# Second gated layer of a two-block transformer kernel on one core: 20 of its 22 feature blocks by seven block products of 256-token halves

## The reference, cut to what matters

```python
def swiglu(h, w1, w3, w2):                     # w1, w3: 1024 x 2816, w2: 2816 x 1024
    return (silu(h @ w1) * (h @ w3)) @ w2
x = x + 0.5 * m_l[2] * swiglu(modulate(rms_norm(x, norm1_w), ...), ffn1_w1, ffn1_w3, ffn1_w2)   # first gated layer
...                                            # token mixing
x = x + 0.5 * m_l[8] * swiglu(modulate(rms_norm(x, norm3_w), ...), ffn2_w1, ffn2_w3, ffn2_w2)   # second gated layer
...                                            # a second block follows
```

## Time and profile before

| | |
|---|---|
| median of 3 runs | 2056.03 us (2053.0 to 2056.21) |
| the profiled execution | 2053.71 us, its span 2051.9 us (1.8 us lie around it) |
| TensorE busy | 95% of the span |
| VectorE, ScalarE, GpSimd busy | 51%, 41%, 41% |
| first gated layer's pairs | about 155 to 550 us |
| norm ahead of the second gated layer | about 969 to 982 us |
| second gated layer | 972.4 to about 1350 us; its last group's down phase ends it |

### The profile page before, as it was taken

The page is one execution under the profiler, slowest core; times in us unless marked ns, Lnnn a source line. Parts: engine busy times, 40 slices in busy tenths (PEclk is TensorE's granted clock), DMA queues, the critical chain, the costliest instruction groups (busy, mean ns, idle before and its releaser), DMA issues.

```text
span 2051.9 us, 25703 instructions
## 1 busy us (share of the span) xinstructions
PE 1945.4 (95%) x9378; PEld 1628.4 (79%) x9378; DVE 1039.4 (51%) x1563; ACT 834.2 (41%) x1276; POOL 836.5 (41%) x414
## 2 busy tenths in 40 slices
PE   4999999999989999889999999999979989999998
PEld 2999999999978875557888888877745767888886
DVE  3879877557457215965213112578985362121124
ACT  4524242434354235552532333446655454232231
POOL 1337574556424321442443443533612324443432
PEclk8999999999999999889999999999989999999999
DMA  8134343433212120002232232322311212232321
GB/s 350 52 134 139 130 163 110 158 143 115 103 62 83 62 71 31 11 21 88 82 112 92 92 108 87 107 98 83 121 44 42 82 51 83 92 113 82 112 82 62
DMA packets 53487, 197.67 MB, mean 96 GB/s; under 512 B 6320, under 2 KB 7056, under 8 KB 51600
## 3 DMA queue, kind: packets, MB, share of 16 engines
q1 hardware_dynamic: 52240, 191.47, 26.6%
q10 hardware_dynamic: 1152, 4.92, 0.7%
HBM read 194.27 MB, written 2.10 MB: 96 GB/s over the span
## 4 chain that ended last, share of the span: by engine, by line
PE 60%; issue 18%; DVE 10%; POOL 7%; ACT 4%; DMA 1%; SPq 0%; POOLq 0%; DVEq 0%; ACTq 0%
PE ps L2276 26%; PE ps L2405 13%; PE ps L2442 8%; POOL wlo L649 6%; PE ps L2290 2%; PE ps L2631 1%; PE ps L2265 1%; PE ps L2264 1%; PE ps L2263 1%; PE ps L2622 1%; PE ps L2789 1%; PE ps L2805 1%; PE ps L2779 1%; DVE ada_prod L1412 1%; DVE rg_h L2178 1%
## 5 line engine op out<-in xcount | busy, mean ns | idle before, releaser
L649 POOL TENSOR_TENSOR wlo<-raw,whi 128x1024 fp32r<-128x1024 f32 x244 | 602.7, 2481 | 991.9 <-ACT whi L702 968.1
L2276 PE MATMUL ps<-h_hi,whi 128*128 128x512 f32 (+2 forms) x992 | 362.3, 380 | 4.5 <-POOL wlo L649 1.8
L702 ACT ACTIVATE whi<-raw 128x1024 fp32r<-128x1024 f32 x244 | 253.1, 1053 | 272.9 <-PE ps L2276 188.3
L2276 PE MATMUL ps<-h_hi,wlo 128*128 128x512 f32 (+2 forms) x992 | 359.7, 377 | 0.0
L2276 PE MATMUL ps<-h_lo,whi 128*128 128x512 f32 (+2 forms) x992 | 359.1, 376 | 0.0
L2276 PEld LDWEIGHTS ps<-h_hi,whi 128*128 128x128 f32 x992 | 182.8, 188 | 43.1 <-issue 8.3
L656 POOL TENSOR_TENSOR wlo<-raw,whi 128x512 fp32r<-128x512 f32 x108 | 160.6, 1501 | 133.2 <-ACT whi L870 132.8
L2276 PEld LDWEIGHTS ps<-h_lo,whi 128*128 128x128 f32 x992 | 182.3, 188 | 33.5 <-issue 1.0
L2276 PEld LDWEIGHTS ps<-h_hi,wlo 128*128 128x128 f32 x992 | 182.4, 188 | 32.7
L2276 PE MATMUL ps<-g_hi,whi 128*128 128x512 f32 x432 | 168.1, 389 | 0.0
L2276 PE MATMUL ps<-g_lo,whi 128*128 128x512 f32 x432 | 168.1, 389 | 0.0
(11 more groups left out here) (476 smaller groups left out, 3690.7 us busy)
## 6 DMA issues: line engine op xcount, KB each, us to landing
raw<-panels SPq DMA_DIRECT2D x280, 512.0 KB, 3.7
ada_w<-ada_t SPq DMA_DIRECT2D x56, 512.0 KB, 3.9
ada_f<-ada_p SPq DMA_DIRECT2D x8, 1024.0 KB, 17.4
x_lat<-x_t SPq DMA_DIRECT2D x1, 2048.0 KB, 7.9
out<-x_lat SPq DMA_DIRECT2D x8, 256.0 KB, 2.2
x_ctx<-ctx_t SPq DMA_DIRECT2D x1, 1024.0 KB, 10.0
cond_b<-cond SPq DMA_DIRECT2D x1, 1024.0 KB, 21.9
x_ctx<-mem_t ACTq DMA_DIRECT2D x1, 1024.0 KB, 4.8
```

The lines of the kernel that those rows point to most:

```text
L649: pool.tensor_tensor(wlo[:, sl], raw[:, sl], whi[:, sl].bitcast(f32), ALU.subtract).then_inc(lo_done, 1)
L702: act.activation(whi[:, sl], raw[:, sl], ACT.Copy).then_inc(hi_done, 1)
L2276: ins = pe.matmul(bank(banks + b, n), wt[:, w], a[:, at_(kc, c0):at_(kc, c0) + n], start=kc == 0 and j == 0, stop=kc == n_k - 1 and j == 2)
```

## The change

Blocks 2 to 21 of the second gated layer go by seven block products of 256-token halves; blocks 0 and 1 (`plain`) stay as they were. What is new beside the reuse of the first layer's functions:

- the norm ahead of the layer also writes the input unrounded, `h32_2` (ScalarE, 8 more instructions), and rounds two panels in its midst;
- VectorE forms differences of token halves from it (16 instructions of 256 columns), ScalarE rounds them (4 of 768), VectorE makes their low parts (4 of 768); another set, `t4_2`, takes the place of the late token halves in `h_hi` and `h_lo` once the plain blocks are done;
- of a block's seven low parts VectorE makes two, 3 and 5 (`vector_low`), and GpSimd five;
- VectorE's additions in the down phases and its work for the later stages are interleaved with weight sums of the next group's first block; the loops are written out.

In the diff `act` is ScalarE, `dve` VectorE, `pool` GpSimd, `pe` TensorE.

```diff
+HALF2 = LAT // 2
+PLAIN2 = 2
+L2_PAIRS = (FF_GROUPS[0] - PLAIN2,) + FF_GROUPS[1:]
+VECTOR_LOW = (3, 5)
...
             def low_operand(m, j):
+                if m >= PAIRS and j in VECTOR_LOW:
+                    pool.wait_ge(s_lo, 6 * m + j)
+                    pool.sem_inc(s_lo, 1)
+                    return
...
-            low_part(2, P_WOUT + 2)
-            low_part(3, P_WOUT + 3)
-            with pool.Fori(P_WOUT // RING + 1, N_PANELS // RING) as i:
+            for p in range(P_WOUT + 2, P_FFN2 + 2 * PLAIN2):
+                low_part(p % RING, p)
+            for n in range(len(L2_PAIRS)):
+                for m in range(PAIR2[n], PAIR2[n] + L2_PAIRS[n]):
+                    for j in range(7):
+                        low_operand(m, j)
+                for d in range(KC):
+                    low_part(d % RING, P_FFN2 + L2_UP[n] + 2 * FF_GROUPS[n] + d)
...
+                    elif m.n == 2 and kc in (3, 4):
+                        q = P_FFN2 + kc - 1
+                        round_panel(q % RING, q // RING + 1, q - RING)
...
+            def second_layer():
...
+                token_sums(0)
+                token_sums(1)
+                plain(0)
+                token_sums(2)
+                token_sums(3)
+                for j in range(3):
+                    round_operand(PAIRS, j)
+                plain(1)
+                act.wait_ge(panel_done, done(P_FFN2 + 2 * PLAIN2 - 1))
+                for e in range(2):
+                    act.activation(late_halves2(h_hi, e), ...).then_inc(t4_rounded, 1)
+                for j in range(3, 7):
+                    round_operand(PAIRS, j)
+                for n in range(len(L2_PAIRS)):
+                    for m in range(PAIR2[n], PAIR2[n] + L2_PAIRS[n]):
+                        pair_products(m)
...
+                    for q in range(down + RING, down + KC):
+                        round_panel(q % RING, q // RING + 1, q - RING)
+                        if q == down + RING:
+                            memory_squares() if n == 0 else memory_hi()
+                    for j in range(7):
+                        round_operand(PAIR2[n + 1], j)
...
+            def vector_low(m, e):
+                j = VECTOR_LOW[e]
+                dve.wait_ge(s_hi, 6 * m + j + 1)
+                dve.tensor_tensor(half_slot(wlo, j), operand(m, j), half_slot(whi, j).bitcast(f32), ALU.subtract).then_inc(v_lo, 1)
...
+            def second_layer():
...
+                differences(0, 2)
+                plain(0)
+                differences(2, 4)
+                weight_sums(PAIRS, 0)
+                sums_low(0)
+                sums_low(1)
+                weight_sums(PAIRS, 1)
+                sums_low(2)
+                sums_low(3)
+                plain(1)
...
+                weight_sums(PAIRS, 2)
+                vector_low(PAIRS, 1)
+                for n in range(len(L2_PAIRS)):
+                    for m in range(PAIR2[n], PAIR2[n] + L2_PAIRS[n]):
+                        if pair_unit(m):
+                            pair_tail(m - 1)
+                        if not last_pair(m):
+                            weight_sums(m + 1, 0)
+                            weight_sums(m + 1, 1)
+                        pair_sums_of(m)
+                        if not last_pair(m):
+                            vector_low(m + 1, 1)
...
             def first_products(m):
...
                 if m == 0:
                     pe.wait_ge(t_ready, 4)
+                elif m == PAIRS:
+                    pe.wait_ge(t_ready, 8)
...
+            def second_layer():
+                cols = token_cols(LAT)
+                first_pair(P_FFN2, (0, 2), H_BEFORE[2], cols)
...
+                for n, g in enumerate(FF_GROUPS):
+                    for m in range(PAIR2[n], PAIR2[n] + L2_PAIRS[n]):
+                        first_products(m)
```

More of the change, by code:

```diff
@@ L50 @@
 PAIRS = FF - L1_SIZES[0]
+HALF2 = LAT // 2
+PLAIN2 = 2
+L2_PAIRS = (FF_GROUPS[0] - PLAIN2,) + FF_GROUPS[1:]
+VECTOR_LOW = (3, 5)
+PAIR2 = [PAIRS + sum(L2_PAIRS[:n]) for n in range(len(L2_PAIRS))]
+PAIRS2 = PAIRS + sum(L2_PAIRS)
+L2_UP = [sum(2 * g + KC for g in FF_GROUPS[:n]) for n in range(len(FF_GROUPS))]
 STAGES = [("f", f) for f in range(L1_SIZES[0])] + [("d", 0)]
@@ L163, in build @@
         t4 = [at(f"t4_{e}", 2 * HALF, R_TMP + (3 + 6 * e) * KB) for e in range(2)]
+        g2_hi = at("g2_hi", 8 * LAT, R_G, f32r)
+        g2_lo = at("g2_lo", 8 * LAT, R_G + 16 * KB, f32r)
+        h32_at = [R_G + (4 + 2 * kc) * KB if kc < 6 else R_G + (28 + 2 * (kc - 6)) * KB for kc in range(KC)]
+        h32_2 = [at(f"h32_2_{kc}", LAT, h32_at[kc]) for kc in range(KC)]
+        t2_hi = [at(f"t2_hi{j}", 3 * HALF2, R_G + (32 + 3 * j) * KB, f32r) for j in range(4)]
+        t2_lo = [at(f"t2_lo{j}", 3 * HALF2, R_MORE + 3 * j * KB, f32r) for j in range(4)]
+        t2_32 = [at(f"t2_32_{j}", 3 * HALF2, R_MORE + 3 * j * KB) for j in range(4)]
+        t4_2 = at("t4_2", 4 * HALF2, R_G + 44 * KB)
         up_b = at("up_b", TOK, R_TMP)
@@ L1505, in norm @@
                         b = (kc % 2) * TOK
-                        if m.n == 0 and kc >= 2:
-                            dve.wait_ge(h32_done, kc - 1)
+                        if m.n in (0, 2) and kc >= 2:
+                            dve.wait_ge(h32_done, (KC if m.n else 0) + kc - 1)
                         for j, (xs, n, c0, _) in enumerate(m.segs()):
@@ L2390, in first_product @@
                 p = pair_panel(m)
-                if j < 6:
+                if m >= PAIRS and j in VECTOR_LOW:
+                    pe.wait_ge(v_lo, 2 * (m - PAIRS) + VECTOR_LOW.index(j) + 1)
+                elif j < 6:
                     pe.wait_ge(s_lo, 6 * m + j + 1)
@@ L2394, in first_product @@
                     pe.wait_ge(lo_done, p + 2)
-                out = bank((bank_x(m), bank_v(m), bank_y(m), bank_x(m), bank_y(m), bank_z(m), bank_v(m))[j], HALF)
+                H = half_tokens(m)
+                S, sums_hi, sums_lo = (LAT, t2_hi, t2_lo) if m >= PAIRS else (TOK, t_hi, t_lo)
+                out = bank((bank_x(m), bank_v(m), bank_y(m), bank_x(m), bank_y(m), bank_z(m), bank_v(m))[j], H)
                 for kc in range(4):
@@ L2926, in _ @@
             norm(norms[2])
-            for G in GROUPS[0:3]:
-                hidden_up(G, H_BEFORE[2])
-                hidden_down(G)
-                if G["n"] == 1:
-                    memory_stats()
+            second_layer()
             input_projection2()
```

196 lines of the change are left out of this document (147 added, 49 removed).

## The result

| | before | after |
|---|---|---|
| median | 2054.52 us (4 runs, 2052.76 to 2056.21) | 2073.9 us (4 runs, 2071.83 to 2076.98) |
| ratio | | 1.0094, 95% interval 1.0081 to 1.0107 |
| profiled execution | 2053.71 us, span 2051.9 | 2074.9 us, span 2072.6 |

The change makes the kernel 19.4 us slower. The page of the kernel after, beside the earlier trace rows: TensorE is busy for about as long as before, but for 94% of a longer span. Its share of the chain that ended last stands at 30% instead of 60%, but the shares after add up to 52% of the span only (before to 100%), so the two can't be compared.

The account below looks back on a forecast made before the run. It took TensorE's pace to bound the kernel now, and the full VectorE-GpSimd port to hold back changed blocks. Profiled 2053.7 + 12.5 (start) + 0.0 (blocks) + 0.3 (rest) = 2066.5, against the runs' median 2068.8; forecast 2068 us, range 2052 to 2080.

Parts of the forecast that it names:

- TensorE's saving: Second layer's blocks: seven products take 10.04 us instead of 10.81, 0.77 us a block, 15.4 for 20, if TensorE never waits.
- The port: Between VectorE and GpSimd: one instruction holds it whole, and the two engines take turns when both wait.
- The block of mid-group: A block in the middle of a group takes 11.05 us, not 10.04, and 0.24 more than now.
- the loop: Mid-group chain from product 6's end through VectorE, GpSimd and ScalarE to the v copy and next product 6: 11.05 us.
- its signs: Expected in the changed profile: among others, TensorE idle about 1 us a mid-group block, ahead of product 6, released by L968.
- the port is full: Mid-group: VectorE's six and GpSimd's five instructions need 9.9 us of the port, against 10.04 of TensorE.
- The first blocks of a group: A group's first block, prepared in the down phase, takes 10.04 us, the second 10.35.
- The last blocks: The last block of each group, with nothing to prepare for, takes 10.8 us.
- the 205.4 of the sum: The 19 blocks behind the first pair block: 205.4 us after the change against 205.4 before, so nothing gained.
- The 0.3 us of the memory root: The memory root's table load of 1.28 us moves ahead of the third group's first silu: +0.3 us.
- The start: From the norm to the first pair block's end: loses 12.5 us, 7.5 of it idle ahead of product 0; 6 to 17.5.
- The rest: Remaining blocks, table loads, down phases and layer end: nothing but +0.3 us for the memory root's load.

Follow-up runs that it names:

- experiment 1: Changed kernel with GpSimd's five low parts a block cut to 32 of 512 columns in the second layer, computation incomplete: 2045.1 us.
- experiment 4: Changed kernel with ScalarE making the next block's y copy before the second rounding to g_hi instead of behind it: 2074.6 us.
- experiment 5: Changed kernel, same instructions, second layer reordered on ScalarE (y copy, v copy, rounding 3 earlier) and VectorE (low part 3 earlier), two waits changed: 2049.0 us.
- experiments 7: Changed kernel with four plain blocks instead of two at the start, and VectorE's token-difference low parts ahead of plain block 1: 2065.2 us.
- 8: Changed kernel with the orders of experiment 5, four plain blocks at the start, and low part 5 of a group's first block earlier: 2047.5 us.
- experiment 2: Changed kernel with all seven low parts of a block on GpSimd and none on VectorE: 2072.1 us.
- 9: 8 with the y copy and the last sum of the first pair block moved ahead: 2040.1 us.

## Why the prediction was right or wrong

It said 2068 us, slower, 2052 to 2080; it is 2073.9, inside the range and the right way. The number is nearer than the steps are: the sum's difference was 12.8 us and the measured one is 19.4, and the median of before that it was added to, 2056.03 us, turned out 1.5 us above that of four runs. By the steps:

- **TensorE's saving** was 0.77 us a block. Measured without waits: 10.00 against 10.88, 0.88 us. The pace of 256 columns was right (10.00/84 = 0.119 us). Before's was not: 222 starts in 50 us counts matmuls that lap over the window's edges. From 986.05 to 1236.39 us there are 1104 of them, 0.2268 us each, 10.88 a block. The estimate by the Trainium skill (TensorE: Matmul & The Clock Gate, Back-to-back issue gap), 109 ns for 256 columns, does not hold here; at 119 the trace is 9% above it. The Trainium skill, in that section, gives the formula for isolated matmuls and says that in a stream with weight loads it is too low for short ones and too high at 512 columns. The prediction left that out, and here it is too low at both, 119 and 227 ns for 109 and 216.
- **The port.** That VectorE with two SBUF inputs and GpSimd shut each other out is shown by experiment 1, that they take turns by the timelines. The Trainium skill (SBUF — State Buffer, Who interferes with whom) calls it an exclusive lock, and these runs agree: 0.68 us against 1.6 to 1.8.
- **The block of mid-group** was 11.05 us and is 11.37. The chain that I wrote down is there instruction by instruction: L1719 behind two of GpSimd's turns, rounding 2, silu, rounding 3, v copy. VectorE's product at 2.34 us after product 6's end is at 2.4, the y copy at 3.43 is at 3.5, sum a11 at 7.70 is at 7.9; each turn took 0.05 to 0.1 more. That is 0.32 us on eleven blocks, 3.5 us, and lies just outside the 0.3 that I gave the method. What the text called the loop, TensorE's product 6 included, was too wide: experiment 4 shows that TensorE isn't in it. Among its signs it put TensorE's idle time ahead of product 6, released by L968; of the 1.4 us a block that TensorE lost, 0.86 stood ahead of product 2, released by L954, and 0.4 ahead of product 6. And its "the port is full" (9.9 of 10.04 us) is not borne out: in experiment 5 the same work fits into 10.00 us, with VectorE waiting for 0.9 us of them.
- **The first blocks of a group** are the step whose mechanism was missing; by size it is a little less than mid-group. I let the second block of a group take 10.35 us, since its first is prepared in the down phase. It takes 11.37 in all three groups, 3.1 us. In the second group's timeline the low part 5 of the first block stands behind VectorE's last addition of the down phase, low part 6 behind that, and low part 0 of the second block behind that, so that the preparation for it starts late; this I did not place. It is a reading and no experiment: no run moves that low part alone, and the first group, which has no down phase ahead, has the 11.37 too. The third group's first block is 11.2 us, not 10.04 and 0.3, 0.8 us. The last blocks are 0.16 longer than the 10.8. With the mid-group's 3.5 us that makes 8.0: the blocks behind the first pair block take 213.4 us for the 205.4 of the sum. Before they take 206.9 for 205.4. Predicted difference 0, measured 6.5. (The 0.3 us of the memory root stand in the sum twice, in the 205.4 and as a term of their own.)
- **The start** was 12.5 us and is 11.8. Product 0 waits 7.5 us (from last start to start) for L1776, product 2 for the y copy, product 6 for the v copy, each at its place to within 0.6 us, counted from the norm's transposes. The clock did fall: products 0 and 1 took 0.213 us a matmul, and the y copy hid it, as written. The window over them:

```profile
1007.00:1013.00 6.00, 5.34 (x24) 5.04 (x24) 5.27 (x8) 3.90 (x8) 1.50 (x1) 0.51 0.00 0
```

- **The rest** was +0.3 and is -0.9: TensorE waited 2.67 us for a panel's low part at the seam to the input projection before, 0.46 after.

Together 12.8 us predicted in the layer and 17.5 measured; 1.9 more of the 19.4 lie outside it. The direction held by the start, the size failed at the blocks. That mid-group would go back to 10.0 us with the same instructions in another order was no case of mine: "the port is full, and the order of the work is fixed" described the kernel's order and was wrong as a bound.

## What to carry to other kernels

When engines feed each other in a ring, look for the one that waits once in a period, and follow that wait back: what its releaser did in the meantime is the list to reorder, and work that needs nothing of the late result goes ahead of it. An engine that waits in several places beside the ring may only show what is left over, as TensorE did here. And an experiment that adds an instruction also moves the signals behind it: look which of the two the time answers to. When a new scheme needs its inputs prepared, count the preparation as a chain and give it as much of the old work as cover; here two more plain blocks at the start, with VectorE's and ScalarE's lists fitted to them, were worth 7.2 us in the layer, and 2.9 once the blocks ran at TensorE's pace.

## What was unexpected of the hardware

VectorE's list became shorter by one instruction more on the port (3.96 us instead of 4.25 for the first sums), because the sums behind it came to lie where GpSimd was waiting. TensorE's clock fell to the lower level for the next 24 matmuls of 256 columns after idle times of 3.8, 3.9, 4.1 and 7.1 us (experiments 7, 8, 1 and the kernel after), so a wait of 3.9 us cost 6.2. Shorter waits did it too: one of 2.1 us ahead of product 2 in experiment 2, for some 16 matmuls, and the 2.67 us at the seam in the kernel before, for 8 of 512 columns, 0.43 us each. Waits of up to 1.3 us among the pair blocks did not (experiments 4 and 9). And the same first 970 us of the program end within a range of 5.4 us from one execution to the next, which is why a difference under some 4 us was read from the layer alone.
